# Products of the 16 meta rows in two passes instead of three, with both halves of the rows side by side as one stationary operand

## What is computed

```python
h = concatenate([meta_tokens, x])                 # 16 + 512 rows
for l in range(2):
    proj = h @ w_in[l]                            # a, g, zc, q, k, v, za, qi, ki, wi
    y_conv = conv_branch(a, g, zc)                # 31 taps, layer norm, gate
    y_attn = sparse_attention(q, k, v, qi, ki, wi, topk=132) * silu(za)
    y = concatenate([y_conv, y_attn]) @ w_out[l]  # 1024 x 1024
    h = layer_norm(alpha * h + y)
return h[16:]
```

## Time and profile before

| | us |
|---|---|
| median of 3 runs | 1113.46 (1112.95 to 1117.24) |
| the profiled execution | 1111.81 |
| its span in the trace | 1110.0 |
| PE busy | 1021.1 (92%) |
| DVE busy | 697.7 (63%) |
| ACT busy | 581.6 (52%) |
| POOL busy | 130.8 (12%) |

### The profile page before, as it was taken

One profiled execution on the slowest core, in us unless ns is written; L12 is line 12 of the kernel. 1 busy time (PEld: TensorE's weight loads), 2 busy tenths in 40 slices (PEclk: granted clock), 3 DMA queues, 4 the chain that ended last, 5 costly groups with the idle time before them and its releaser, 6 DMA issues.

```text
span 1110.0 us, 16657 instructions
## 1 busy us (share of the span) xinstructions
PE 1021.1 (92%) x6484; PEld 868.8 (78%) x6484; DVE 697.7 (63%) x1553; ACT 581.6 (52%) x938; POOL 130.8 (12%) x185
## 2 busy tenths in 40 slices
PE   7998899778999899989989898969999999999997
PEld 7987898766677799879887666758888778877885
DVE  3999999785465559999978755562841333332522
ACT  6584781546543548458437544462484555565331
POOL 0000100101121200010001121124300000000001
PEclk9998999889899999989999989999999999999999
DMA  8775674454300767547528523295767644547661
GB/s 287 182 175 172 156 184 115 125 103 114 66 12 18 210 136 195 123 118 173 114 83 188 136 50 89 68 236 117 224 153 175 167 119 110 138 96 167 164 157 76
DMA packets 23822, 152.36 MB, mean 137 GB/s; under 512 B 2865, under 2 KB 3377, under 8 KB 6849
## 3 DMA queue, kind: packets, MB, share of 16 engines
q0 software_dynamic: 9648, 68.75, 33.4%
q1 hardware_dynamic: 14096, 82.55, 20.9%
HBM read 149.20 MB, written 2.10 MB: 136 GB/s over the span
## 4 chain that ended last, share of the span: by engine, by line
PE 77%; ACT 9%; DVE 6%; DMA 5%; issue 3%; POOL 0%; POOLq 0%; DVEq 0%; SPq 0%; ACTq 0%
PE psum_B L1176 20%; PE psum_A L1176 14%; PE psum_B L1209 9%; PE psum_A L1209 9%; PE psum_A L1330 6%; DMA w_lo<-in_weights 3%; DVE conv_acc L1626 2%; PE psum_C L1232 2%; ACT w_hi L613 2%; PE psum_B L1288 2%; PE psum_A L1542 2%; ACT w_lo L614 2%; PE psum_B L1330 2%; PE psum_B L1542 2%; DMA w_raw<-in_weights 2%
## 5 line engine op out<-in xcount | busy, mean ns | idle before, releaser
L1626 DVE SCALAR_TENSOR_TENSOR conv_acc<-u,vec,conv_acc 128x528 f32<-128x528 f32 (+1 forms) x240 | 173.4, 758 | 3.2
L1176 PE MATMUL psum_B<-x_hi,w_hi 128*128 128x264 f32 (+3 forms) x512 | 147.4, 327 | 10.7 <-ACT shifted L668 5.8
L1176 PE MATMUL psum_B<-x_lo,w_hi 128*128 128x264 f32 (+3 forms) x512 | 144.0, 320 | 0.0
L1176 PE MATMUL psum_B<-x_hi,w_lo 128*128 128x264 f32 (+3 forms) x512 | 143.4, 319 | 0.0
L1011 POOL DMA_DIRECT2D w_lo<-in_weights x67 | 59.3, 886 | 677.0 <-ACT w_lo L614 677.0
L613 ACT ACTIVATE w_hi<-w_raw 128x2048 fp32r<-128x2048 f32 (+2 forms) x87 | 129.5, 1489 | 14.3 <-DMA w_raw<-in_weights 13.9
L614 ACT ACTIVATE w_lo<-w_raw 128x2048 fp32r<-128x2048 f32 (+2 forms) x87 | 128.9, 1481 | 0.0
L1176 PE MATMUL psum_A<-x_hi,w_hi 128*128 128x264 f32 (+2 forms) x496 | 119.2, 298 | 8.2 <-DVE za L1743 4.0
L1176 PE MATMUL psum_A<-x_lo,w_hi 128*128 128x264 f32 (+2 forms) x496 | 116.8, 293 | 0.0
L1176 PE MATMUL psum_A<-x_hi,w_lo 128*128 128x264 f32 (+2 forms) x496 | 116.6, 293 | 0.0
L1176 PEld LDWEIGHTS psum_B<-x_hi,w_hi 128*128 128x128 f32 (+1 forms) x512 | 90.3, 192 | 20.0 <-issue 14.0
(11 more groups left out here) (324 smaller groups left out, 2098.0 us busy)
## 6 DMA issues: line engine op xcount, KB each, us to landing
w_raw<-in_weights SPq DMA_DIRECT2D x67, 1024.0 KB, 5.3
w_lo<-in_weights POOLq DMA_DIRECT2D x65, 1024.0 KB, 8.2
x_first<-in_x_t SPq DMA_DIRECT2D x4, 528.0 KB, 7.0
h<-in_x SPq DMA_DIRECT2D x1, 2048.0 KB, 9.8
out<-h SPq DMA_DIRECT2D x4, 512.0 KB, 2.6
post_ln_g<-in_post_ln_g SPq DMA_DIRECT2D x2, 512.0 KB, 4.2
post_ln_b<-in_post_ln_b SPq DMA_DIRECT2D x2, 512.0 KB, 5.6
w_raw<-in_weights SPq DMA_DIRECT2D x2, 288.0 KB, 5.3
```

The costliest lines, as they stand in the source:

```text
L1176: mm = pe.matmul(ps[0:cols, i, 0:b - a], w[wp][:, kt, at:at + cols], x[xp][:, kt, a:b], start=(kt == 0 and wp + xp == 0), stop=(kt == KD - ...
L1626: got = dve.scalar_tensor_tensor(dst, src, w, dst, ALU.mult, ALU.add)
```

## The change

For tile 0 the hi and lo columns of the activations are copied side by side into a new tile (`pair_meta`, 32 columns each: the 16 meta rows and 16 more that nobody uses). One matmul with these 64 columns as stationary operand and the hi weights gives hi*hi in PSUM rows 0 to 31 and lo*hi in rows 32 to 63; a second with the 32 hi columns and the lo weights adds hi*lo to rows 0 to 31 (`meta_product`). A product is then 8 kt x 2 = 16 matmuls. The two row groups of the result are added at the end: for the values ACT copies both out and POOL adds them; for the output projection DVE adds the second group to the residual with an instruction of its own. In layer 1 only the values have this product.

New waits: PE waits for the copies of ACT; the copies for the output projection wait for the lo parts that POOL makes (`part_lo`); POOL waits for ACT's copy of the values; PE's first product with the values and DVE's fourth item wait for POOL's add (the second half of the values lies for a while in `exps3`).

```diff
+META_AT = ((20, "attn"), (22, "conv"))
...
+    if l == 0:
+        for i, part in META_AT:
+            todo["act"][i].append(("meta", part))
...
+        meta_pair = [sb("meta_hi_lo_in", [P, KD, 64], F32R, at=E_AT + 8 * L), sb("meta_hi_lo_out", [P, KD, 64], F32R, at=WIT_AT)]
...
             def take_v(l, t):
                 use = (l, "v", t)
                 ps = full(use)
-                act.activation(v[0:SIZE[t], t, :], ps[0:SIZE[t], 0, :], ACT.Copy).then_inc(act_took.mark(use), 1)
+                got = act.activation(v[0:SIZE[t], t, :], ps[0:SIZE[t], 0, :], ACT.Copy)
+                if t == 0:
+                    got = act.activation(e[3][0:META, 0:DC], ps[32:32 + META, 0, :], ACT.Copy)
+                got.then_inc(act_took.mark(use), 1)
                 next_blocks(use)
...
+            def pair_meta(step, pair_, ks):
+
+                act.activation(pair_[:, ks, 0:32], xhi[:, ks, 0:32], ACT.Copy)
+                act.activation(pair_[:, ks, 32:64], xlo[:, ks, 0:32], ACT.Copy) \
+                    .then_inc(meta_paired.mark(step), 1)
...
                 for name in ("q", "k"):
                     for c in range(CT):
                         take_channels(l, name, c)
+                    if name == "q":
+                        pair_meta((l, "v"), meta_pair[0], slice(0, KD))
...
+                        elif op[0] == "meta":
+                            part = op[1]
+                            for t in (0, 1):
+                                act.wait_ge(part_lo.sem, part_lo.at((l, part, t)))
+                            pair_meta((l, part), meta_pair[1], slice(0, CT) if part == "conv" else slice(CT, KD))
...
+                pool.wait_ge(act_took.sem, act_took.at((l, "v", 0)))
+                pool.tensor_tensor(v[0:META, 0, :], v[0:META, 0, :], e[3][0:META, 0:DC], ALU.add) \
+                    .then_inc(pool_step.mark((l, "v", 0)), 1)
...
+            def meta_product(ps, pair_, kt, whi_, wlo_):
+
+                if kt < KD - 1:
+                    pe.matmul(ps[0:64, :], pair_[:, kt, :], whi_, start=kt == 0, stop=False)
+                mm = pe.matmul(ps[0:32, :], pair_[:, kt, 0:32], wlo_, start=False, stop=False)
+                if kt == KD - 1:
+                    mm = pe.matmul(ps[0:64, :], pair_[:, kt, :], whi_, start=False, stop=True)
+                return mm
...
                 for kk in range(4):
                     kt = half * 4 + kk
+                    if t == 0:
+                        mm = meta_product(ps, meta_pair[1], kt, w[0][:, kk, :], w[1][:, kk, :])
+                        continue
...
-                for t in TILES:
+                meta_values(l)
+                for t in MAIN:
...
-                dve.scalar_tensor_tensor(dst, dst, ALPHA, ps[0:n, 0, :], ALU.mult, ALU.add) \
-                    .then_inc(dve_took.mark(use), 1)
+                got = dve.scalar_tensor_tensor(dst, dst, ALPHA, ps[0:n, 0, :], ALU.mult, ALU.add)
+                if t == 0:
+
+                    got.then_inc(dve_step.mark((l, "meta", half)), 1)
+                    dve.wait_ge(dve_step.sem, dve_step.at((l, "meta", half)))
+                    got = dve.scalar_tensor_tensor(dst, dst, 1.0, ps[32:32 + n, 0, :], ALU.mult, ALU.add)
+                got.then_inc(dve_took.mark(use), 1)
```

More of the change, by code:

```diff
@@ L405, in build @@
         wit = sb("w_idx_t", [P, L])
+        E_AT = where[0]
         e = [sb(f"exps{i}", [P, L]) for i in range(4)]
@@ L493, in build @@
         small_made = signal("small_made")
+        meta_paired = signal("meta_paired")
         u_made = signal("u_made")
@@ L1211, in rows, with meta_values @@
                 mm.then_inc(psum_full.mark(use), 1)
+            def meta_product(ps, pair_, kt, whi_, wlo_):
[5 more added lines that the diff above has]
+                return mm
+            def meta_values(l):
+                use = (l, "v", 0)
+                ps = claim(use, next_buf("AB"))[:, 0, :]
+                pe.wait_ge(meta_paired.sem, meta_paired.at((l, "v")))
+                for half in range(2):
+                    w = [part[:, :].rearrange("p (k c) -> p k c", k=4) for part in weights(NUMBER[(l, "v", 0)] + half)]
+                    for kk in range(4):
+                        mm = meta_product(ps, meta_pair[0], 4 * half + kk, w[0][:, kk, :], w[1][:, kk, :])
+                mm.then_inc(psum_full.mark(use), 1)
             def index_weights(l):
@@ L1278, in probs_times_v @@
                 pe.wait_ge(act_took.sem, act_took.at((l, "PT", t, hd + 1)))
+                if i == 0:
+                    pe.wait_ge(pool_step.sem, pool_step.at((l, "v", 0)))
                 for j in [0] + list(range(1, t + 1)):
@@ L1323, in output_half @@
                 part = ("conv", "attn")[half]
-                for tt in ((0, 1) if t == 0 else (t,)):
-                    pe.wait_ge(part_lo.sem, part_lo.at((l, part, tt)))
+                pe.wait_ge(part_lo.sem, part_lo.at((l, part, t)))
                 w = [block_[:, :].rearrange("p (k c) -> p k c", k=4) for block_ in weights(NUMBER[(l, "wo", n, half)])]
+                if t == 0:
+                    pe.wait_ge(meta_paired.sem, meta_paired.at((l, part)))
                 for kk in range(4):
                     kt = half * 4 + kk
+                    if t == 0:
+                        mm = meta_product(ps, meta_pair[1], kt, w[0][:, kk, :], w[1][:, kk, :])
+                        continue
                     for wp, xp in PASSES:
@@ L1715, in masked_logits @@
                     dve.wait_ge(psum_full.sem, psum_full.at((l, "PT", *items[l][i - 4])))
+                elif i == 3:
+                    dve.wait_ge(pool_step.sem, pool_step.at((l, "v", 0)))
                 a = SCORE_AT[t] if t else MASK0_AT
```

## The result

| | before | after |
|---|---|---|
| median of the first runs, us | 1113.28 (4 executions) | 1105.06 (1103.89 to 1106.83) |
| ratio, 95% interval | | 0.9919 (0.9893 to 0.9946) |
| profiled execution / its span, us | 1111.81 / 1110.0 | 1106.83 / 1105.0 |
| all executions of the study, mean, us | 1114.4 (85) | 1106.2 (17) |

The change is faster by 8.1 +- 1.0 us over all executions of the two kernels, 0.7%. The prediction said 1114.5, with 1107.0 as its lower end: it was wrong, and on the faster side. One execution of the kernel before, of 5485.79 us, is left out of all these figures.

What follows compares the result with a forecast made beforehand. PE, busy 1021.1 of 1110.0 us, was taken as the bound. Products +0.36, copies +0.41 and +0.25 summed to +1.0 us, median 1114.5 from 1113.46; range 1107.0 to 1119.5.

Steps and rivals of the forecast that it cites:

- What bounds the kernel: Whole kernel: PE is busy 1021.1 of 1110.0 us; a matmul less pays only where PE is what all wait for.
- first rival: All four products: going from 64 to 32 columns costs nothing; -5.7 us, median 1107.8, 0.5% faster; chance 0.20.
- A change to 64 columns costs 0.14, to 32 columns 0.11: Inside `meta_product`: seven changes each way between 64- and 32-column operands add 1.75 us, so a product takes 5.46.
- second rival: All four products: narrow forms stream rounded operands at float32 rate; 13.4 us more, median 1128, 1.3% slower; chance 0.08.
- Leaving and entering: At the ends of tile 0's products: changing from 128 columns to 64 costs 0.14 us, back to 128 columns 0.19.
- The copies: ACT's pair copies for the output: 0.41 us at item 20 and 0.25 at item 22; the values' pair is hidden.
- attn: Pair of ACT copies for the output at item 20, ahead of item 21's transposes, on the chain: +0.41 us.
- conv: Pair of ACT copies at item 22 behind the tanh, ahead of the left output product: +0.25 us with the hand-over.
- The pair for the values: ACT copies between q and k, 0.63 us, hidden by ACT's 2.21 us of idle time before k.
- the second copy of the values: On ACT: 0.5 to 0.6 us, hidden by ACT's 1.5 us of idle time each tile.
- POOL's addition: POOL's add for the values has until the masks at 193.65, 30 us later; waits for it cost nothing.
- DVE's second addition: With each residual of tile 0: 0.67 us, DVE late by 0.4, covered by 5.7 us, so nothing.

## Why the prediction was wrong, by its own steps

- What bounds the kernel: right for the output, where the 16 matmuls less arrive at full price. For the values the first rival took the idle time of DVE as the cap of layer 0, 1.06. The gain is 1.05, but that agreement is luck: the limit was ACT's buffer, and DVE's idle time before the logits varies with the execution (1.06 and 1.58 in layer 0 of the two traces of before, 2.48 and 1.23 in layer 1).
- "A change to 64 columns costs 0.14, to 32 columns 0.11": this step failed, and with it the sum. The size is right for plain float32 (0.26 measured for both together, 0.25 forecast) and nil for rounded operands. The narrow matmuls in the rows behind it were plain float32; I had written that all 64-wide matmuls of the trace were float32, but used it only to leave the second rival open, not to doubt the main price. The step put 1.75 us of changes into each product; the runs show none. A product takes 3.72 us, not 5.46, four of them 7 us less than forecast, of which some 1.7 don't arrive at the values.
- Leaving and entering (0.19 and 0.14): nothing to be seen on entering the values (156.53, 156.78 and 157.01, starts 0.25 and 0.23 apart) and behind the output (0.23). Only coming from the float32 products with the values, the first distance is 0.28 instead of 0.23.
- The copies: "attn" 0.41 forecast, 0.40 measured, on the chain where it was put. "conv" 0.25 forecast; PE waited 0.34 and 0.35 for it in two other forms of the change and not at all in the traces of the changed kernel itself. The estimate from rows of other sizes (0.21 for a copy of 128 numbers) was good: 0.20.
- The pair for the values, the second copy of the values, POOL's addition: hidden, as said; no engine waits for them in the traces. DVE's second addition took 0.68, forecast 0.67, and the next residual follows without idle time, late and covered, as said.
- First rival (0.20): its mechanism is what happened. Its terms were -1.06, -1.5, -3.8 and +0.66; the stages show -1.05, -1.0, -3.7 and +0.4. Only layer 1's values were sized too high. ACT's buffer was rightly named as their limit, but the old end, 161.82, was read in the chain, whose pieces start later than the matmuls do. In the order of time tile 1 starts 5.57 us behind tile 0 in the kernel before and 4.28 to 4.30 after, 1.27 to 1.29 less, not 1.5, and 1.0 of it reaches the logits. Its 1107.8 is 1.5 us above the median of the changed kernel's 17 executions (1106.3).
- Second rival (rounded operands at the rate of float32 in narrow form): ruled out, 0.23 us a matmul.
- The range ended at 1107.0, 0.8 below the first rival, which had no room for its own spread: single profiled executions differ by more than that, and the rival's sum had none of what the stages don't show.

## What to carry to other kernels

A price belongs to the form it was read on: operand type as well as shape. When every row behind a price has one type and the change has the other, that difference is the first rival and not a footnote. And look at what is queued behind a wait for a DMA. ACT's wait of 2 us stood here ahead of a take that PE needed, PE was idle for 3.8 us, and the granted clock fell behind that; moving one entry of the schedule brought 3 to 4 us, while the change took 32 matmuls out to bring 8.

## What the runs showed of the hardware that I had not expected

- Rounded matmuls of 128 rows with 64, 48, 32 and 16 columns at the array's first columns take turns at 0.23 us with no extra. Plain float32 ones pay 0.26 for a change from 64 to 32 columns and back.
- Plain float32 matmuls, 64 columns wide, into columns 0 to 63 and 64 to 127 run at once: 0.42 us for both instructions together (0.43 for one alone).
- Between the values' first matmul and DVE's first logits lie 39.75 to 39.77 us in eight of eight stages without the change, while the executions of the kernel before differ by up to 14 us (1106.56 to 1120.65). The spread lies elsewhere. It goes with the mean granted clock, 5.5 us for each 0.01.
